# Scores of two differential heads in one group of matmuls, dilated projections cut into six halves, on one Trainium2 core

## The chip, the cores and the metric

The kernel runs on one core of one Trainium2 chip. The metric is the device time of one execution in microseconds (us): the median of several executions, beside which one execution was recorded by the hardware profiler. All times below of "the trace" come from that one recorded execution.

## What is computed

One decoder block over 256 tokens of width 1024 (all float32): attention with sixteen heads of two kinds, and then a mixture of 32 experts with the top four chosen for each token. Cut to what matters here:

```
h = rms_norm(x); proj = h @ w_in                      # 1024 x 3072
dq, dk, dv, lq, lk, lv = split(proj)                  # six parts of 512 columns
# eight differential heads: two score maps each, contraction over 32
s = q[h, m] . k[h, m] / sqrt(32) - slope * dist ; causal
p = softmax(s[m=0]) - lam * softmax(s[m=1]) ; o = p @ dv ; rms_norm(o)
# eight dilated heads: one map each, contraction over 64, three dilations mixed
o = mixture(softmax(lq . lk)) @ lv
x = x + mix @ w_out
x = x + moe(rms_norm(x))    # 32 experts: gate/up 1024 x 2048, down 1024 x 1024
return rms_norm(x)
```

The expert weights are 32 x 12.6 MB; every one of them is read once.

## The kernel before, in words

**Stages.** After the normalised input is turned (`hT`), TensorE makes the query/key part of the differential heads (`project(DQK, k)`, k from 0 to 7), then the differential values (`DV`). Then a loop over steps g = 0 to 15 runs heads 0 to 7 (differential) and 8 to 15 (dilated), with the rest of the projections (`EQ`, `EK`, `EV`: the dilated queries, keys and values) and later pieces of the output projection put between the small matmuls of the heads as filling. After step 15 come the rest of the output projection, the router and the experts, two experts to a round.

**One step on TensorE** (the loop near the end of the attention part of the TensorE program). Step g turns the probabilities of head g-1 (`turn_probs`, three transposes), makes the scores of head g+1 (`score(g + 1)`, for the differential heads), does its filling from the table `FILL`, turns a pair of mixed heads where g is 4, 6, 8 or 10 (`turn_mix`), and multiplies the probabilities of head g-1 with the values (`pv`). A step is named below by its g.

**The scores.** `score(g)` makes the two maps m = 0, 1 of one head. A map has 256 query rows in two parts: the later 128 against 256 keys and the earlier 128 against 128 keys. Its operands lie in 32 partitions, 64*(g % 2) + 32*m and on, so the two maps use two of the four groups of 32 rows of the array; they go to banks 4 and 5 of PSUM, for every head. Dilated heads go in twos already (`score_pair`: two heads, 64 partitions each, banks 4 and 5).

**VectorE, iteration g:** `negated_scores(g + 1)` reads the scores of the next head out of PSUM, adds the distance term and takes the row minimum; `diff_probs(g)` normalises the exponentials of head g and subtracts the second map; then come odd tasks: `rest_of_bias(1)` and `bias_part(1)` (two long operations that split the expert biases into bf16 parts, in iterations 1 and 2; their end, `bias_split`, lets the load queue start the loads of `w_out`), `keep_qk` (copies two finished 128x256 pieces of a projection out of PSUM with the scale), and `norm_pair` in iterations 3, 5, 7, 9 (normalises a pair of heads before `turn_mix`; it has one operation on GpSimd in its middle).

**ScalarE, iteration g:** `turn_probs(g - 1)` copies the turned probabilities, `exps(g + 1)` makes the exponentials, `keep_mixT` copies the turned pair, `keep_pv` the head's output. For g of 4, 6 and 8 `keep_mixT` stands after `exps(g + 1)`. On TensorE `pv` of the same step waits for that copy (`mixT_ready`), since both use bank 7.

**The load queue (SyncE)** issues all weight loads in the order of the program, each after a wait for its buffer. `gu_ring` has sixteen slots; during attention `w_in` lies in slots 0 to 11 and `hT`, `qkT`, `vS` in 12 to 15. The loads of the first two experts' gate/up weights go in eight steps s, which wait in order: dqk_used 2 and 4, then (after `bias_split` and the loads of `w_out`) eq_used 2 and 4, ev_used 2 and 4, ev_used 4 with scores_done 8, and, for s = 7, all scores, the turned pairs and the values' use. After it come the first down weights, which wait for the output projection.

## Time and profile before

| what | us |
|---|---|
| median of 3 executions (lowest, highest) | 1057.95 (1056.53, 1058.64) |
| the profiled execution | 1058.58 |
| its span in the trace | 1056.9 |
| TensorE matmul busy | 1037.4 |
| VectorE / ScalarE / GpSimd busy | 231.4 / 118.0 / 21.6 |
| moved by the DMA engines | 423.87 MB, 401 GB/s over the span |

The span is the time between the first and the last record of the core; 1.7 us of the execution lie around it. Matmuls overlap in the array, so the start of one record to the start of the next tells what a matmul costs, and not its length. Each float32 matmul of the program stands in the trace as two records of the same shape. In the views "<-" behind a wait names what ended it.

### The profile page before, as it was taken

How to read it: one execution, taken by the hardware profiler on the slowest of the kernel's cores; microseconds unless marked ns; L12 is line 12 of the kernel's file. 1: busy time of each engine (PE TensorE's matmuls, PEld its weight loads, DVE VectorE, ACT ScalarE, POOL GpSimd, SP SyncE). 2: the span in 40 equal slices, each digit the busy share in tenths (PEclk: the TensorE clock that was granted, in tenths of full speed). 3: DMA queues.
4: the chain of work that ended last, by engine and by line, in shares of the span. 5: the costliest groups of instructions: out<-in, count | busy, mean ns of one | idle time of the engine just before them, and what ended most of it. 6: DMA issues, size and time to landing. Idle time of an engine off the chain costs nothing.

```text
span 1056.9 us, 13197 instructions
## 1 busy us (share of the span) xinstructions
PE 1037.4 (98%) x5569; PEld 464.8 (44%) x5569; DVE 231.4 (22%) x515; ACT 118.0 (11%) x275; POOL 21.6 (2%) x39
## 2 busy tenths in 40 slices
PE   8999999999999999999999999999999999999997
PEld 7686544434343433434343434343433434343432
DVE  3567543121111111112121211111111111121111
ACT  1133420010000000000000000000000000000001
POOL 1000410000000000000000000000000000000000
PEclk9999999999999999999999999999999999999999
DMA  9946669999999999999999999999999999999996
GB/s 289 417 180 245 235 267 380 426 428 427 434 430 432 431 430 429 434 434 429 433 430 434 429 433 432 434 429 434 430 434 428 434 430 434 425 425 429 427 422 258
DMA packets 28027, 423.87 MB, mean 401 GB/s; under 512 B 5392, under 2 KB 5408, under 8 KB 11008
## 3 DMA queue, kind: packets, MB, share of 16 engines
q1 hardware_dynamic: 25680, 422.80, 94.7%
q10 hardware_dynamic: 2320, 0.67, 0.3%
q8 instruction: 21, 0.34, 0.1%
q14 instruction: 6, 0.05, 0.0%
HBM read 422.41 MB, written 1.05 MB: 401 GB/s over the span
## 4 chain that ended last, share of the span: by engine, by line
PE 90%; DVE 7%; ACT 1%; issue 1%; DMA 1%; SPq 0%; DVEq 0%; POOL 0%
PE psum L953 42%; PE psum L1001 15%; PE psum L1023 7%; PE psum L673 6%; PE psum L915 5%; PE psum L1040 4%; PE psum L788 3%; PE psum L648 3%; PE psum L678 2%; DVE mixed L1448 2%; DVE mixed L1444 2%; DVE mixed L1446 2%; ACT mixed L580 1%; PE psum L939 1%; DMA gu_ring<-in_w_in_dram 1%
## 5 line engine op out<-in xcount | busy, mean ns | idle before, releaser
L953 PE MATMUL psum<-gu_ring,mixed 128*64 128x512 f32 x2048 | 446.1, 593 | 0.0
L953 PEld LDWEIGHTS psum<-gu_ring,mixed 128*64 128x64 f32 x2048 | 143.4, 137 | 280.8 <-issue 275.7
L1444 DVE TENSOR_SCALAR mixed<-psum 128x512 f32<-128x512 f32 x32 | 22.1, 692 | 379.7 <-PE psum L953 379.7
L1001 PE MATMUL psum<-dn_ring,mixed 128*64 128x512 f32 x352 | 78.0, 595 | 3.8 <-ACT mixed L580 3.8
L1001 PE MATMUL psum<-mixed 128*64 128x512 f32 x352 | 78.0, 595 | 0.0
L1401 DVE TENSOR_TENSOR mixed<-posm,iota 128x256 f32<-128x256 f32 x47 | 20.0, 425 | 258.8 <-PE psum L648 258.5
L934 PE MATMUL psum<-mixed 64*128 64x512 f32 x256 | 63.6, 615 | 0.7 <-ACT mixed L584 0.7
L598 ACT ACTIVATE mixed<-psum 128x512 f32<-128x512 f32 x30 | 17.9, 597 | 402.1 <-PE psum L953 402.1
L673 PE MATMUL psum<-gu_ring 128*128 128x256 f32 x256 | 59.2, 389 | 1.8 <-DMA gu_ring<-in_w_in_dram 1.8
L915 PE MATMUL psum<-mixed,xres 128*128 128x128 f32 x480 | 57.4, 278 | 0.0
L915 PEld LDWEIGHTS psum<-mixed,xres 128*128 128x128 f32 x480 | 55.0, 192 | 0.7
L673 PEld LDWEIGHTS psum<-gu_ring 128*128 128x128 f32 x256 | 49.1, 195 | 9.7 <-issue 2.5
L584 ACT ACTIVATE mixed<-psum 128x512 f32<-128x512 f32 x32 | 19.1, 597 | 274.4 <-PE psum L1001 191.9
L1040 PE MATMUL psum<-ident,mixed 128*64 128x64 f32 x704 | 47.1, 286 | 2.0
L1001 PEld LDWEIGHTS psum<-dn_ring,mixed 128*64 128x64 f32 x352 | 25.1, 137 | 52.3 <-issue 52.3
L1040 PEld LDWEIGHTS psum<-ident,mixed 128*64 128x64 f32 x704 | 44.1, 216 | 8.5 <-DVE mixed L1448 8.5
L1001 PEld LDWEIGHTS psum<-mixed 128*64 128x64 f32 x352 | 24.3, 137 | 45.3 <-issue 44.0
L934 PEld LDWEIGHTS psum<-mixed 64*128 64x128 f32 x256 | 22.0, 186 | 41.8 <-issue 40.2
L1023 PE MATMUL psum<-dn_ring,mixed 128*64 128x512 f32 x160 | 35.4, 595 | 0.5
L1023 PE MATMUL psum<-mixed 128*64 128x512 f32 x160 | 35.4, 595 | 0.5 <-ACT mixed L580 0.5
L1414 DVE TENSOR_TENSOR mixed<-psum,prm 128x512 f32<-128x512 f32 x28 | 19.4, 692 | 69.6 <-PE psum L915 69.6
L648 PEld LDWEIGHTS psum<-ident,mixed 128*128 128x128 f32 (+1 forms) x163 | 19.3, 160 | 34.8 <-issue 28.9
(162 smaller groups left out, 546.5 us busy)
## 6 DMA issues: line engine op xcount, KB each, us to landing
gu_ring<-in_w_gate_up_dram SPq DMA_DIRECT2D x44, 4096.0 KB, 34.2
gu_ring<-in_w_gate_up_dram SPq DMA_DIRECT2D x35, 2048.0 KB, 18.9
dn_ring<-in_w_down_dram SPq DMA_DIRECT2D x11, 4096.0 KB, 31.7
mixed<-in_w_down_dram SPq DMA_DIRECT2D x11, 4096.0 KB, 31.4
dn_ring<-in_w_down_dram SPq DMA_DIRECT2D x9, 2048.0 KB, 17.5
mixed<-in_w_down_dram SPq DMA_DIRECT2D x8, 2048.0 KB, 16.0
gu_ring<-in_w_in_dram SPq DMA_DIRECT2D x11, 1024.0 KB, 17.7
gu_ring<-in_w_gate_up_dram SPq DMA_DIRECT2D x9, 1024.0 KB, 8.5
```

The source lines that it names most:

```text
L648: return nc.tensor.transpose(dst, src, ident[0:rows, 0:rows])
L673: last = mm(bank[b][:, c:c + T], w[:, P * (m0 + m):P * (m0 + m + 1)], hT[:, k, :], start=(k == 0 and m % 2 == 0), stop=(k == KT - 1), skip ...
L678: last = mm(bank[b0 + a][:, :], hT[:, k, P * a:P * (a + 1)], w[:, v0:v0 + 512], start=(k == 0), stop=(k == KT - 1))
L788: last = mm(bank[2 * a + c][:, :], mixT[:, kt, P * a:P * (a + 1)], dn_ring[:, kt // 2, w0:w0 + 512], start=(kt == 0), stop=(kt == KT - 1))
L915: last = mm(bank[b][:, c:c + P], rows, sel[:, a, :, :].rearrange("p e n -> p (e n)"), start=(a == 0), stop=(a == TT - 1))
L934: last = mm(bank[(0, 5)[a] + c][:, :], combT[rows, P * a:P * (a + 1)], yrow[rows, :], start=False, stop=True, skip_group_check=True)
L953: last = mm(bank[b0 + b][CAP * c:CAP * (c + 1), :], xg[:, k, CAP * half:CAP * (half + 1)], gu_ring[:, 8 * half + k, w0:w0 + 512], start=Fa ...
L1001: last = mm(bank[4][CAP * c:CAP * (c + 1), :], actT[:, CAP * k:CAP * (k + 1)], dn_whole[half][:, k // 2, w0:w0 + 512], start=False, stop=( ...
L1023: last = mm(bank[4][CAP * c:CAP * (c + 1), :], actT[:, a0:a0 + CAP], dn_slot[slot][:, k // 2 % 2, w0:w0 + 512], start=False, stop=(k == KT ...
L1040: last = mm(bank[7][rows, CAP * k:CAP * (k + 1)], act_t.rearrange("n (p k) -> n k p", k=KT)[:, k, :], ident[:, rows], start=True, stop=True)
L1444: chain(V.tensor_scalar(up_t, bank[b0 + 1][:, :], 1.0 - LIMIT, 1.0 + LIMIT, ALU.max, ALU.min))
L1446: chain(V.scalar_tensor_tensor(out=up_t, in0=bank[b0][:, :], scalar=LIMIT, in1=up_t, op0=ALU.min, op1=ALU.mult))
```

## The change

Scores: `score(g)` is replaced by `score_maps(g)`, which makes heads g and g+1 (g even) in one go: four maps at partitions 0, 32, 64 and 96, the even head in banks 4 and 5, the odd one in banks 2 and 3, first the four wide parts and then the four narrow ones. It is called before `DV` 2 for heads 0 and 1, and in steps 1, 3 and 5. `score_maps(0)` waits for all four `keep_qk` of the differential part. `negated_scores` reads banks 2 and 3 for odd heads.

Projections: `EQ`, `EK` and `EV` are each cut into two halves h (two of four pieces, or one of two token blocks), all eight k of a half before the other half, half 0 in bank 0 and half 1 in bank 1; banks 2 and 3 are no longer used by them. A unit of filling is half a k; the units per step are 8, 6, 6, 6, 6, 4, 6, 6 for steps 1 to 8, twice the former numbers. The matmuls are the same in number and size. VectorE copies the four halves of `EQ` and `EK` one by one in iterations 2, 3, 4 and 6 (before: two in 4, two in 6), in iteration 3 ahead of `norm_pair`.

Biases: `rest_of_bias(1)` and `bias_part(1)` both go to iteration 0 of VectorE; in iteration 1 it waits for its own probabilities there.

Mix: ScalarE does every `keep_mixT` ahead of `exps(g + 1)`.

```diff
-        FILL = {0: [(DV, k) for k in range(4, KT)], 1: [(EQ, 2), (EQ, 3)], 2: [(EQ, 4), (EQ, 5), (EQ, 6)],
-                3: [(EQ, 7), (EK, 0), (EK, 1)], 4: [(EK, 2), (EK, 3), (EK, 4)], 5: [(EK, 5), (EK, 6), (EK, 7)],
-                6: [(EV, 0), (EV, 1)], 7: [(EV, 2), (EV, 3), (EV, 4)], 8: [(EV, 5), (EV, 6), (EV, 7)]}
+        HALVES = [(c, h, k) for c in (EQ, EK, EV) for h in range(2) for k in range(KT)]
+        FILLED = (0, 0, 8, 14, 20, 26, 32, 36, 42, 48)
...
-                if g in TURN_AT and g > NH:
+                if g in TURN_AT:
                     keep_mixT(TURN_AT[g])
                 if g + 1 < 2 * NH:
                     exps(g + 1)
                 if g == 0:
                     keep_v(dv_done, 1, 6, 0)
-                if g in TURN_AT and g <= NH:
-                    keep_mixT(TURN_AT[g])
...
+            def project_half(chunk, h, k):
+
+                g = (1, 2, 2)[chunk]
+                w = gu_ring[:, 4 * g + k // 2, D * (k % 2):D * (k % 2) + D]
+                if chunk == EK and h == 0 and k % 2 == 0:
+                    pe.wait_ge(w_in_in[4 * g + k // 2], 16)
+                if k == 0:
+                    pe.wait_ge(qk_ready, ((1, 3), (5, 6), (7, 8))[chunk][h])
+                if chunk == EV:
+                    last = mm(bank[h][:, :], hT[:, k, P * h:P * (h + 1)], w[:, 512:D], start=(k == 0), stop=(k == KT - 1))
+                else:
+                    for m in range(2):
+                        c = (512, 0)[chunk] + P * (2 * h + m)
+                        last = mm(bank[h][:, T * m:T * (m + 1)], w[:, c:c + P], hT[:, k, :], start=(k == 0 and m == 0),
+                                  stop=(k == KT - 1), skip_group_check=True)
+                if h == 1 and chunk != EK:
+                    if k % 2:
+                        last.then_inc({EQ: eq_used, EV: ev_used}[chunk], 1)
+                elif k == KT - 1:
+                    last.then_inc(half_done, 1)
...
-            def score(g):
-                if g in (0, 4):
-                    pe.wait_ge(qk_ready, {0: 2, 4: 4}[g])
-                if g >= 1:
+            def score_maps(g):
+
+                if g == 0:
+                    pe.wait_ge(qk_ready, 4)
+                else:
                     pe.wait_ge(scores_read, g)
-                h = g % NH
-                for m in range(2):
-                    r0 = HD * (h % 2) + DK * m
-                    q, k = qkT[r0:r0 + DK, h // 2, :], qkT[r0:r0 + DK, 4 + h // 2, :]
-                    mm(bank[4 + m][:, 0:T], q[:, P:T], k, start=True, stop=True)
-                    last = mm(bank[4 + m][:, T:T + P], q[:, 0:P], k[:, 0:P], start=True, stop=True)
-                last.then_inc(scores_done, 1)
+                maps = [(bank[(4, 2)[i] + m], HD * i + DK * m) for i in range(2) for m in range(2)]
+                q, k = qkT[:, g // 2, :], qkT[:, 4 + g // 2, :]
+                for b, r in maps:
+                    mm(b[:, 0:T], q[r:r + DK, P:T], k[r:r + DK, :], start=True, stop=True)
+                for i, (b, r) in enumerate(maps):
+                    last = mm(b[:, T:T + P], q[r:r + DK, 0:P], k[r:r + DK, 0:P], start=True, stop=True)
+                    if i % 2:
+                        last.then_inc(scores_done, 1)
...
-            score(0)
-            project(DV, 2)
-            project(DV, 3)
+            score_maps(0)
+            for k in range(2, KT):
+                project(DV, k)
             for g in range(2 * NH):
+                fill = HALVES[FILLED[g]:FILLED[g + 1]] if g <= NH else []
                 if g == 1:
-                    pe.wait_ge(qk_ready, 3)
-                    project(EQ, 0)
-                    project(EQ, 1)
+                    for chunk, h, k in fill[0:4]:
+                        project_half(chunk, h, k)
+                    fill = fill[4:]
                 if g >= 1:
                     turn_probs(g - 1)
-                if g + 1 < NH:
-                    score(g + 1)
+                if g % 2 and g + 1 < NH:
+                    score_maps(g + 1)
                 elif g % 2 and g + 1 < 2 * NH:
                     score_pair(g + 1)
...
-                maps, b = (2, 4) if g < NH else (1, 4 + g % 2)
+                maps, b = (2, 4 - 2 * (g % 2)) if g < NH else (1, 4 + g % 2)
...
+                if g == 0:
+                    rest_of_bias(1)
+                    bias_part(1).then_inc(bias_split, 1)
                 if g == 1:
-                    rest_of_bias(1)
+                    dve.wait_ge(probs_ready, g + 1)
                 if g == 2:
-                    bias_part(1).then_inc(bias_split, 1)
                     dve.wait_ge(sub_in, 16 * 2)
                     V.tensor_scalar(prm[:, 16:17], prm[:, 16:17], 1.0 - LAM_INIT, None, ALU.mult).then_inc(sub_ready, 1)
-                if g == NH - 2:
-                    dve.wait_ge(ek_done, 1)
-                    for h in range(2):
-                        keep_qk(12 + 2 * h, 2 + h, 1.0)
+                if g in (2, 3, 4, 6):
+                    h = (2, 3, 4, 6).index(g)
+                    if h == 1:
+                        dve.wait_ge(eq_used, 4)
+                    else:
+                        dve.wait_ge(half_done, (1, 0, 2, 3)[h])
+                    keep_qk(8 + 2 * h, h % 2, HD ** -0.5 if h < 2 else 1.0)
                 if g >= 3 and g % 2 == 1 and g <= NH + 1:
                     norm_pair((g - 3) // 2)
-                if g == 4:
-                    dve.wait_ge(eq_used, 4)
-                    for h in range(2):
-                        keep_qk(8 + 2 * h, h, HD ** -0.5)
```

## Rows read from the trace of the kernel before

**Rows 1.** Busy time by stretch: stretch, us, busy PE PEld DVE ACT POOL, PEclk, DMA share, GB/s

```profile
42.00:112.00 70.00, 69.39 (x333) 49.21 (x333) 45.10 (x109) 24.71 (x88) 6.04 (x7) 1.00 0.62 254
...
124.60:139.50 14.90, 14.90 (x68) 7.27 (x67) 7.74 (x34) 4.95 (x13) 6.61 (x10) 1.00 0.01 2
139.50:163.00 23.50, 22.73 (x132) 11.99 (x134) 12.96 (x46) 4.39 (x11) 1.14 (x2) 1.00 0.90 358
182.00:1026.00 844.00, 836.77 (x4614) 341.51 (x4612) 129.92 (x244) 65.88 (x127) 0.00 (x0) 1.00 1.00 430
```

**Rows 2.** TensorE's records in order: start, length, line, shape, count; one round

```profile
801.18 13.95 PE L953 MATMUL psum<-gu_ring,mixed 128*64 128x512 f32 x64
...
857.71 0.65 PE L953 MATMUL psum<-gu_ring,mixed 128*64 128x512 f32 x2
```

**Rows 3.** Waits of the weight loads, 900 us to the end: in total, times, longest

```profile
PEld psum L953 <- DMA gu_ring<-in_w_gate_up_dram: 1.9, 4, 0.7
```

**Rows 4.** The load queue's issues in order of time

```profile
72.18 2.04 SPq L299 DMA_DIRECT2D dn_ring<-in_w_out_dram  x4
...
139.52 0.33 SPq L281 DMA_DIRECT2D gu_ring<-in_w_gate_up_dram  x1
...
162.25 2.04 SPq L331 DMA_DIRECT2D gu_ring<-in_w_gate_up_dram  x2
```

**Rows 5.** TensorE's records in order, steps 5 to 8 of the attention

```profile
85.10 0.50 PE L648 MATMUL psum<-ident,mixed 128*128 128x128 f32 x3
85.53 0.71 PE L720 MATMUL psum<-gu_ring 32*128 32x256 f32 x4
86.06 0.39 PE L721 MATMUL psum<-gu_ring 32*128 32x128 f32 x4
86.39 5.45 PE L673 MATMUL psum<-gu_ring 128*128 128x256 f32 x24
...
92.28 0.50 PE L648 MATMUL psum<-ident,mixed 128*128 128x128 f32 x3
...
95.61 1.88 PE L678 MATMUL psum<-gu_ring 128*128 128x512 f32 x4
98.10 0.41 PE L754 MATMUL psum<-gu_ring,mixed 128*128 128x64 f32 x2 [0.61 <-ACT mixed L528]
...
98.79 0.50 PE L648 MATMUL psum<-ident,mixed 128*128 128x128 f32 x3
...
105.94 0.50 PE L648 MATMUL psum<-ident,mixed 128*128 128x128 f32 x3
106.27 1.88 PE L678 MATMUL psum<-gu_ring 128*128 128x512 f32 x4
```

**Rows 6.** TensorE's records of the router, four groups of 32 columns

```profile
146.43 0.67 PE L845 MATMUL psum<-mixed 128*32 128x128 f32 x16
147.02 1.13 PE L788 MATMUL psum<-dn_ring,mixed 128*128 128x512 f32 x2
```

**Rows 7.** VectorE's records in order, iterations 1 and 2

```profile
59.27 0.95 DVE L1211 SCALAR_TENSOR_TENSOR mixed<-mixed,psum 128x768 f32<-128x768 f32 x1 [7.79 <-PE psum L721]
...
63.15 3.35 DVE L1183 TENSOR_TENSOR dn_ring<-dn_ring,mixed 32x3072 f32<-32x3072 f32 x1
...
70.41 1.75 DVE L1188 CAST mixed<-dn_ring 32x3072 bf16<-32x3072 f32 x1
```

**Rows 8.** VectorE's records in order, iterations 5 and 6

```profile
86.51 0.95 DVE L1211 SCALAR_TENSOR_TENSOR mixed<-mixed,psum 128x768 f32<-128x768 f32 x1 [2.37 <-PE psum L721]
...
92.47 0.42 DVE L1259 TENSOR_TENSOR mixed<-mixed,st 128x256 f32<-128x256 f32 x1 [1.12 <-POOL st L432]
93.70 0.95 DVE L1211 SCALAR_TENSOR_TENSOR mixed<-mixed,psum 128x768 f32<-128x768 f32 x1 [0.81 <-PE psum L721]
...
97.19 0.35 DVE L1229 SCALAR_TENSOR_TENSOR mixed<-mixed,st 128x128 f32<-128x128 f32 x1
97.46 1.28 DVE L1176 SCALAR_TENSOR_TENSOR gu_ring<-psum,mixed 128x512 f32<-128x512 f32 x2
```

More of the change, by code:

```diff
@@ L241, in moe_block @@
         PAIR_AT = {11: 4, 13: 5, 15: 6}
[L242 to L245 removed]
+        DQK, DV = range(2)
+        EQ, EK, EV = range(3)
+        HALVES = [(c, h, k) for c in (EQ, EK, EV) for h in range(2) for k in range(KT)]
+        FILLED = (0, 0, 8, 14, 20, 26, 32, 36, 42, 48)
         OUT = {9: [(0, 1), (0, 0)], 10: [(1, 0)], 11: [(2, 0)], 12: [(3, 0)], 13: [(1, 1)], 14: [(4, 0)], 15: [(5, 0)]}
@@ L666, in project @@
                     pe.wait_ge(w_in_first[k], 16)
-                elif chunk in (DQK, DV, EK) and k % 2 == 0:
+                elif k % 2 == 0:
                     pe.wait_ge(w_in_in[s], 16)
-                if chunk in (DQK, EQ, EK):
-                    b0, m0, n = {DQK: (0, 0, 8), EQ: (0, 4, 4), EK: (2, 0, 4)}[chunk]
-                    for m in range(n):
-                        b, c = b0 + m // 2, T * (m % 2)
-                        last = mm(bank[b][:, c:c + T], w[:, P * (m0 + m):P * (m0 + m + 1)], hT[:, k, :],
+                if chunk == DQK:
+                    for m in range(KT):
+                        b, c = m // 2, T * (m % 2)
+                        last = mm(bank[b][:, c:c + T], w[:, P * m:P * (m + 1)], hT[:, k, :],
@@ L674, in project @@
                                   start=(k == 0 and m % 2 == 0), stop=(k == KT - 1), skip_group_check=True)
+                    if k % 2:
+                        last.then_inc(dqk_used, 1)
                 else:
-                    b0, v0 = {DV: (6, 0), EV: (0, 512)}[chunk]
                     for a in range(TT):
-                        last = mm(bank[b0 + a][:, :], hT[:, k, P * a:P * (a + 1)], w[:, v0:v0 + 512],
-                                  start=(k == 0), stop=(k == KT - 1))
-                if chunk in (DQK, EQ, EV) and k % 2:
-                    last.then_inc({DQK: dqk_used, EQ: eq_used, EV: ev_used}[chunk], 1)
@@ L682, in project @@
-                if chunk == DV and k == KT - 1:
-                    last.then_inc(dv_done, 1)
-                if chunk == EK and k == KT - 1:
-                    last.then_inc(ek_done, 1)
+                        last = mm(bank[6 + a][:, :], hT[:, k, P * a:P * (a + 1)], w[:, 0:512], start=(k == 0),
+                                  stop=(k == KT - 1))
+                    if k == KT - 1:
+                        last.then_inc(dv_done, 1)
+            def project_half(chunk, h, k):
[13 more added lines that the diff above has]
+                if h == 1 and chunk != EK:
+                    if k % 2:
+                        last.then_inc({EQ: eq_used, EV: ev_used}[chunk], 1)
+                elif k == KT - 1:
+                    last.then_inc(half_done, 1)
@@ L800, in _ @@
             project(DV, 1)
-            score(0)
-            project(DV, 2)
-            project(DV, 3)
+            score_maps(0)
+            for k in range(2, KT):
+                project(DV, k)
             for g in range(2 * NH):
+                fill = HALVES[FILLED[g]:FILLED[g + 1]] if g <= NH else []
                 if g == 1:
-                    pe.wait_ge(qk_ready, 3)
-                    project(EQ, 0)
-                    project(EQ, 1)
+                    for chunk, h, k in fill[0:4]:
+                        project_half(chunk, h, k)
+                    fill = fill[4:]
                 if g >= 1:
                     turn_probs(g - 1)
-                if g + 1 < NH:
-                    score(g + 1)
+                if g % 2 and g + 1 < NH:
+                    score_maps(g + 1)
                 elif g % 2 and g + 1 < 2 * NH:
                     score_pair(g + 1)
-                for i, (chunk, k) in enumerate(FILL.get(g, ())):
-                    if k == 0:
-                        pe.wait_ge(qk_ready, {EK: 4, EV: 6}[chunk])
-                    project(chunk, k)
-                    if i == 0 and g in TURN_AT:
+                for i, (chunk, h, k) in enumerate(fill):
+                    project_half(chunk, h, k)
+                    if i == 1 and g in TURN_AT:
                         turn_mix(TURN_AT[g], g)
```

6 lines of the change are left out of this document (2 added, 4 removed).

## The prediction

> **What bounds the kernel now.** I read the busy time by stretch first. From 42 to 112 us, where the heads and projections run, TensorE is busy for 69.39 of 70 us at the full clock, and VectorE for 45 [rows 1]: what is taken off TensorE's list there is time. Then the question is whether the end follows. From 182 to 1026 us both TensorE (836.8 of 844) and the DMA engines (share 1.00, 430 GB/s) are full [rows 1]. A round of two experts reads 2 x 12.58 = 25.17 MB, which is 58.5 us at 430 GB/s; TensorE's rounds are 857.71 - 801.18 = 56.5 us apart [rows 2]. So the stream of weights is slower by 2.0 us a round and uses up the lead that it had, and after 900 us weight loads begin to wait for data (1.9 us in four waits) [rows 3]. The end is therefore the start of the stream plus its bytes. Where does the stream start? From 124.6 to 139.5 us the DMA engines stand still (share 0.01) [rows 1]; the next load is issued at 139.52 and waits for TensorE's scores, turned pairs and values, and those behind it up to 162.25 wait for TensorE's output projection and first expert [rows 4]. So a microsecond that TensorE saves before 139 us is saved in both, and only such a one.
>
> **Scores, eight times two maps against four times four.** Step 5 begins with turned probabilities at 85.10 and scores at 85.53, and its filling starts at 86.39: 1.29 us. Step 8 has no scores, and its filling starts 106.27 - 105.94 = 0.33 us after its beginning [rows 5]. One call of scores thus costs 0.96 us, two calls 1.92. What would four maps together cost? Filling records of 256 columns come at about 0.22 us each, transposes of 128 columns at 0.11 (three in 0.33) [rows 5]. A call has four records of 256 and four of 128 columns, 1.32 us if one ran after the other; the 0.96 is half of it (0.66) and 0.30 for entering and leaving. So two groups of 32 rows already run at once. Four maps are 2.64 us of records: 0.66 + 0.30 = 0.96 with four at once (and some 0.03 for two more starts), 1.32 + 0.30 = 1.62 with two at once, 2.94 with one at a time. The trace has no four groups of rows. Its nearest row is the router's sixteen records of 128 columns in four groups of columns: 1.76 us in series, 147.02 - 146.43 = 0.59 us in fact, which is four at once (0.44) and 0.15 [rows 6]. There the four write different partitions; here they write the same partitions in four banks, as the two do now in two banks. I take four at once, 0.99 us: 4 x (1.92 - 0.99) = **3.7 us saved**. The bounds are 1.2 us saved (two at once) and 4.1 us lost (one at a time).
>
> The Trainium skill (TensorE: Matmul & The Clock Gate, section "Measured speedup vs the span model") gives 3.07 times for four row tiles with a contraction over 32 and 512 columns. By it a group would be 2.64 / 3.07 + 0.30 = 1.16 us and the saving an estimated 3.0 us; no run here shows that yet.
>
> **Mix copied sooner.** In step 6 the last filling starts at 95.61, four records of 0.43 us, so `pv` could start at 97.33; it starts at 98.10, after a wait for ScalarE's copy of the turned pair (L528) [rows 5], which stands behind the exponentials. With the copy first, 0.8 us goes. The exponentials are then later by the wait for the turn, in steps 4, 6 and 8. They are those of head g+1, whose probabilities are turned in step g+2; a step is 4.7 to 7.2 us, and this delay some 3. No cost. Bounds: 0 (the next wait is as late) and 0.8.
>
> **Halves.** The records are the same in number and shape, and each step has the same amount of filling: zero on TensorE. New are the waits. Each half's first k waits for a copy of the same bank, made one to three iterations before (qk_ready 5 in iteration 2, used in the middle of step 3; 6 in 3, used late in step 4; 7 in 4, used in step 6). VectorE in turn waits for a half in iterations 2, 3, 4 and 6, with `norm_pair` and the next scores queued behind it, and TensorE's `turn_mix` behind those. In iteration 3 the half's last record is 1.7 us into the filling and VectorE comes to the wait some 5 us after its scores, so that costs nothing but the copy's 0.65 us ahead of `norm_pair`; `turn_mix` has over 0.5 us left. The load queue now gets eq_used and ev_used from the second half alone. Its loads of s = 4 to 6 are then issued between 103 and 108 us, and they land long before 135 us, since the engines idle now from 124.6 us [rows 1]. Zero, within 0.3 us both ways.
>
> **Biases.** 3.35 + 1.75 us of VectorE [rows 7] go to iteration 0. They are hidden by the 7.79 us in which it waits for the scores of head 2 [rows 7]; without that cover they would push head 1's probabilities and cost up to 5 us. The loads of `w_out` are issued at about 57 us and not at 72.18 [rows 4]; nobody waits for them. Taking them out of iterations 1 and 2 gives nothing on TensorE. `score_maps(0)` waits for four copies and not two; that is 1.28 us more at most [rows 8], and two k of `DV` (eight records of 0.43, 3.4 us) stand before it on TensorE to cover all four. Zero.
>
> **What is late next.** The shorter steps must still find their probabilities. The tight place is step 7. Count from step 5's beginning, 85.10: VectorE begins with the scores at +1.41 and ends `norm_pair` at 92.89 = +7.79; head 6's probabilities take 97.54 - 93.70 = 3.84 more: +11.65 [rows 8]. TensorE needs 7.2 for step 5 and 6.51 - 0.96 - 0.8 = 4.75 for step 6, +11.95 [rows 5]. The fourth copy (half of 1.28 us, begun 3.76 after the scores, +12.2) is wanted by `score_pair(8)` at +12.4 [rows 8]. Both hold by 0.2 to 0.3 us, about a semaphore's way; I take off 0.1 us. In iteration 4 and 6 VectorE needs no new scores, so it is earlier there than now.
>
> **The sum.** 3.7 + 0.8 - 0.1 = 4.4 us. The profiled execution took 1058.58 us (0.6 above the median of 1057.95), of which 1054.2 remain; against the median that is 1053.6 us. All steps from 7 on, the stream and the end move by the same amount, since each is released by TensorE.
>
> **Rivals.** (A) Only two groups of rows run at once: 1.2 + 0.8 - 0.1 = 1.9 us, **1056.1**. For it: no row shows more than two row groups. The Trainium skill (PSUM — Partial Sum Buffer, section "PSUM: the matmul accumulator") says that TensorE's only way out is one write port to PSUM; read strictly that would forbid even the two banks at once of now. Chance 0.14. (B) The hand-offs come due: VectorE is late by about 1 us at the beginnings of steps 2 and 7, where its margin is 0.2 us: 2.4 us remain, **1055.6**. Against it: two of its iterations are about 11 us of work and TensorE's two steps 13. Chance 0.08. (C) TensorE is earlier but the stream isn't, because a load behind 139.52 is bound to something that doesn't move: the 2 us a round eat the gain, **1058.0**. The idle 14.9 us speak against it [rows 1]. Chance 0.06. (D) Slower: the four groups block each other at PSUM and run one after the other. Then a group is 2.94 us, 4 x 1.02 = 4.1 lost, 0.8 won: **1061.3**. It turns the sign once a group is over 2.1 us, and is beyond 0.2% slower from 2.65. The two at once of now speak against it. Chance 0.04. The forecast has 0.68.
>
> **Chances and range.** 0.2% is 2.1 us, about what can be told from no change. The forecast is faster by more in nearly all its cases (0.67), A in under half (0.06), B mostly (0.06): faster 0.79. Within: the rest of these and C, 0.16. Slower: D and a remainder, 0.05. The range goes from 1052.4 (the forecast less the 1.2 us by which the executions differ) to 1056.8 (A with its spread); it leaves C and D out.
>
> **What would show it.** Right: four records of 256 columns within some 50 ns of each other, a group of scores under 1.1 us from its first record to the filling, four such groups; no wait for L528 in step 6 and step 6 near 4.7 us; step 8 begins near 101.5 (now 105.94); the load of 139.52 issued near 135.1; the same 430 GB/s and the same round after it. Wrong: a group of 1.6 us or more; idle time of TensorE before the probabilities of head 1 or 6, or in front of `score_pair(8)`; a load issue between 135 and 160 us that kept its time.

## The result, and the profile after

| | before | after |
|---|---|---|
| median, us (lowest, highest; executions) | 1057.28 (1056.53, 1058.64; 4) | 1051.76 (1051.32, 1052.05; 4) |
| the profiled execution | 1058.58 | 1052.05 |
| its span | 1056.9 | 1050.3 |
| first score record | 42.10 | 40.31 |
| step 9 begins | 112.26 | 105.43 |
| load of s = 7 is issued | 139.52 | 132.70 |

The ratio of after to before is 0.995 [0.9938, 0.9962]: 5.5 us faster, where 4.4 was forecast; the time lies 0.6 us under the range. The seven loads before s = 7 come earlier too.

The comparison of two profiled executions holds more than the change. The first score record starts 1.8 us earlier (42.10 and 40.31), and nothing ahead of it was changed. What the change does is counted from there: from the first score to the beginning of step 9 it was 70.16 us and is 65.12, so **5.04 us** less. The experiments below show that both pass on to the end, the sum of the two meeting the difference of the spans to within 0.4 us.

Stretches of after (columns as in [rows 1], whose stretches these are):

```profile
42.00:112.00 70.00, 70.00 (x344) 49.23 (x343) 48.05 (x123) 28.27 (x96) 7.51 (x9) 1.00 0.66 268
124.60:139.50 14.90, 14.90 (x57) 7.13 (x56) 5.21 (x18) 4.07 (x9) 3.79 (x7) 1.00 0.39 144
182.00:1026.00 844.00, 836.80 (x4614) 341.53 (x4610) 129.89 (x244) 65.25 (x126) 0.00 (x0) 1.00 1.00 430
```

TensorE has no idle time left among the heads (70.00 of 70). The DMA engines' gap has moved forward, so that they are at work again before 139.5. From 182 to 1026 us the two kernels' lines are nearly the same: TensorE has the same 4614 records and 836.8 us, the DMA engines move the same 430 GB/s, and only ScalarE's time differs by 0.6 us. Nothing was gained or lost there.

TensorE's records of after in order (start, length, line, shape, count), steps 1 to 3:

```profile
55.04 0.49 PE L646 MATMUL psum<-ident,mixed 128*128 128x128 f32 x3
55.46 0.71 PE L734 MATMUL psum<-gu_ring 32*128 32x256 f32 x8
55.99 0.40 PE L736 MATMUL psum<-gu_ring 32*128 32x128 f32 x8
56.32 3.72 PE L693 MATMUL psum<-gu_ring 128*128 128x256 f32 x16
...
60.49 0.50 PE L646 MATMUL psum<-ident,mixed 128*128 128x128 f32 x3
60.83 5.35 PE L693 MATMUL psum<-gu_ring 128*128 128x256 f32 x24
66.01 0.33 PE L770 MATMUL psum<-gu_ring,mixed 128*128 128x64 f32 x2
...
66.62 0.49 PE L646 MATMUL psum<-ident,mixed 128*128 128x128 f32 x3
67.05 0.71 PE L734 MATMUL psum<-gu_ring 32*128 32x256 f32 x8
```

L734 and L736 are the wide and the narrow parts of `score_maps`. Eight wide records take 0.71 us from the first one's start to the last one's end, as long as four did in step 5 of before. The first records of the four maps' wide parts start within 0.02 us of each other (55.456 to 55.476). The group takes 56.32 - 55.46 = 0.86 us up to the filling, as a call of two maps did (86.39 - 85.53 = 0.86) [rows 5]. Four maps cost what two cost. Step 2, now without scores, is 6.13 us long and was 7.18. The other steps with a call taken out went from 7.41 to 6.36 (step 4) and from 6.51 to 4.61 (step 6); steps 1, 3, 5, 7 and 8 kept their length to within 0.02.

The same view of after, steps 6 and 7:

```profile
87.35 0.50 PE L646 MATMUL psum<-ident,mixed 128*128 128x128 f32 x3
87.69 1.88 PE L689 MATMUL psum<-gu_ring 128*128 128x512 f32 x4
89.41 0.38 PE L646 MATMUL psum<-ident,mixed 128*128 128x128 f32 x2
89.62 1.88 PE L689 MATMUL psum<-gu_ring 128*128 128x512 f32 x4
91.34 0.33 PE L770 MATMUL psum<-gu_ring,mixed 128*128 128x64 f32 x2
...
91.96 0.50 PE L646 MATMUL psum<-ident,mixed 128*128 128x128 f32 x3
92.39 0.70 PE L747 MATMUL psum<-gu_ring 64*128 64x256 f32 x4
```

`pv` (L770) starts 1.72 us after the last filling's beginning, which is its four records of 0.43, without the wait for L528 that stood there before [rows 5]. In step 7 the turned probabilities of head 6 and the scores (L747) follow at once: neither has an idle time in front. The margin is small, though. One of the waits of TensorE's weight loads from 40 to 112 us of after (in total, times, longest):

```profile
PEld psum L747 <- DVE gu_ring L1191: 0.2, 1, 0.2
```

The weight load of these scores waited 0.2 us for VectorE's copy of the last half of `EK`; it runs beside the matmuls, so nothing was lost.

The load queue (start of the first, time to the end of the last, count):

```profile
101.36 31.67 SPq L281 DMA_DIRECT2D gu_ring<-in_w_gate_up_dram  x4
134.54 0.33 SPq L290 DMA_DIRECT2D dn_ring<-in_w_down_dram  x1
```

The four issues are those of s = 4 to 7; the last begins at 101.36 + 31.67 - 0.33 = 132.70, 6.8 us earlier than the 139.52 of [rows 4], and the span ends 6.6 us earlier.

### The profile page after: what moved, and what is told of

Same layout as the page of the kernel before. It is cut to its first block, busy times and chain, and to the rows that moved or that the text cites. A ratio compares the mean times of both kernels' runs of the same rounds, so it can differ in the third digit from the quotient of the medians.

```text
span 1050.3 us, 13196 instructions
## 1 busy us (share of the span) xinstructions
PE 1032.3 (98%) x5569; PEld 461.9 (44%) x5569; DVE 231.3 (22%) x515; ACT 118.0 (11%) x275; POOL 21.6 (2%) x39
## 3 DMA queue, kind: packets, MB, share of 16 engines
HBM read 422.41 MB, written 1.05 MB: 403 GB/s over the span
## 4 chain that ended last, share of the span: by engine, by line
PE 86%; DVE 6%; DMA 5%; SPq 1%; ACT 1%; issue 1%; DVEq 0%; POOL 0%
PE psum L968 40%; PE psum L1016 15%; PE psum L1038 5%; PE psum L930 5%; PE psum L1055 5%; DMA gu_ring<-in_w_gate_up_dram 4%; PE psum L804 3%; PE psum L693 3%; PE psum L669 3%; PE psum L646 2%; DVE mixed L1463 2%; DVE mixed L1459 2%; DVE mixed L1461 2%; PE psum L689 1%; PE psum L675 1%; SPq L384 1%
## 5 line engine op out<-in xcount | busy, mean ns | idle before, releaser
L646 PE MATMUL psum<-ident,mixed 128*128 128x128 f32 (+1 forms) x163 | 31.7, 294 | 1.5 <-DVE mixed L1345 0.5
L954 PE MATMUL psum<-mixed 96*64 96x512 bf16 x192 | 32.7, 392 | 0.0
```

The lines of the kernel that those rows point to most:

```text
L646: return nc.tensor.transpose(dst, src, ident[0:rows, 0:rows])
L954: return mm(bank[b][CAP * c:CAP * (c + 1), :], bias_sel[half][0:3 * NE, :], bias3[0:3 * NE, col:col + 512], start=True, stop=False, skip_g ...
```

## Experiments: does it repeat, and what is each part worth?

Each result is given with the kernel before, run in turn with it on the same chip; all changes are to the changed kernel, unless said. "Heads" is the time from the first score record to the beginning of step 9 in the profiled execution, "start" the time from the span's beginning to that record.

| run | median, us | ratio to before | span | start | heads |
|---|---|---|---|---|---|
| before (profile of the start) | | | 1056.9 | 42.10 | 70.16 |
| e0 changed | 1051.13 | 0.9948 [0.9935, 0.9962] | 1049.3 | 39.57 | 65.13 |
| e10 changed again | 1051.50 | 0.9954 [0.9940, 0.9967] | 1049.4 | 39.66 | 65.12 |
| e1 head by head | 1051.53 | 0.9948 [0.9933, 0.9964] | 1051.8 | 41.97 | 65.18 |
| e2 mix late | 1054.20 | 0.9972 [0.9960, 0.9984] | 1052.5 | 41.80 | 66.11 |
| e3 one head a step | 1055.65 | 0.9993 [0.9984, 1.0002] | 1053.4 | 39.42 | 69.27 |
| e4 biases late | 1052.47 | 0.9961 [0.9945, 0.9976] | 1050.5 | 39.56 | 66.35 |
| e5b extra in step 6 | 1054.72 | 0.9981 [0.9972, 0.9990] | 1052.9 | 39.59 | 68.56 |
| e6 less gather | 1051.32 | 0.9954 [0.9940, 0.9967] | 1049.3 | 39.96 | 65.13 |
| e7 filler | 1051.86 | 0.9953 [0.9940, 0.9967] | 1049.4 | 39.73 | 65.13 |
| e9 more filler | 1052.06 | 0.9956 [0.9942, 0.9969] | 1051.2 | 41.14 | 65.14 |
| e8 mix sooner alone (on before) | 1056.18 | 0.9997 [0.9988, 1.0006] | 1053.9 | 39.54 | 69.75 |

**The changed kernel once more.**

> The changed kernel again, beside the kernel before on the same chip. Two theories of the 5.5 us between the medians (and 6.6 between the two spans). Theory 1: the heads' part gives 4.9 us (in the two traces, from the first record of DV to the beginning of step 9: 112.26 - 38.57 = 73.7 before, 105.59 - 36.95 = 68.6 or a little more after), and the rest, up to 1.8 us, lies before the first changed line and comes and goes between executions: in the trace of before TensorE's granted clock is 0.5 from 8.5 to 12.0 us, in that of after it is not. Then executions of one kernel fall into two groups some 1.7 us apart, each with its clock share (about 0.997 against 0.999), and like against like the change is 4.9 to 5.2 us. Theory 2: the change itself moves the start; then all executions of this kernel start fast and all of the kernel before start slow, and the difference is 6.6 us in each round.

Measured: 1051.13 us (1051.05 to 1051.69) beside 1056.64 for the kernel before (17 executions, 1056.14 to 1057.37). The heads took the same 65.1 us, but the start was 39.57 and not 40.31, and the span 1049.3.

Between the profile of before and this one the span differs by 7.6 us: 42.10 - 39.57 = 2.53 of it is the start, and 70.16 - 65.13 = 5.03 the heads. The two terms add up to the whole. In the runs below the same sum comes out to within 0.4 us. None of the executions of either kernel here is late, and their medians still differ by 5.5 us; of this the trace explains the 5.03 of the heads, and the rest is inside the interval of the ratio. So the theory that the change itself moves the start is out: before's code also starts at 39.54 (e8).

**The order of the maps in the queue.** Here head g's eight records are issued before head g+1's.

```diff
-                for b, r in maps:
-                    mm(b[:, 0:T], q[r:r + DK, P:T], k[r:r + DK, :], start=True, stop=True)
-                for i, (b, r) in enumerate(maps):
-                    last = mm(b[:, T:T + P], q[r:r + DK, 0:P], k[r:r + DK, 0:P], start=True, stop=True)
-                    if i % 2:
-                        last.then_inc(scores_done, 1)
+                for pair in (maps[0:2], maps[2:4]):
+                    for b, r in pair:
+                        mm(b[:, 0:T], q[r:r + DK, P:T], k[r:r + DK, :], start=True, stop=True)
+                    for b, r in pair:
+                        last = mm(b[:, T:T + P], q[r:r + DK, 0:P], k[r:r + DK, 0:P], start=True, stop=True)
+                    last.then_inc(scores_done, 1)
```

> The same sixteen records of a group, but the two maps of the even head first (wide, then narrow) and then those of the odd head. If the array takes whatever rows are free out of its queue, the two heads still overlap and a group costs 0.9 us: 0 us against the changed kernel. If only neighbours in the program run at once, two maps run at a time and a group costs some 0.65 us more: 4 x 0.65 = 2.6 us slower than the changed kernel (about 1054.3 where that has 1051.7).

Measured: 1051.53 us; heads 65.18. TensorE's records of this kernel, step 1:

```profile
57.12 0.73 PE L735 MATMUL psum<-gu_ring 32*128 32x256 f32 x8
57.66 0.41 PE L737 MATMUL psum<-gu_ring 32*128 32x128 f32 x8
58.00 2.21 PE L693 MATMUL psum<-gu_ring 128*128 128x256 f32 x9
```

A group is 58.00 - 57.12 = 0.88 us, 0.02 more than in the order of the change. So the order of the maps is worth next to nothing as long as the sixteen records stand together. What a matmul of another kind between the two heads' maps would do, no run shows. The span, 1051.8, is 2.5 longer than e0's, and 2.40 of it is a later start, not the order.

**Mix copied late again.**

```diff
-                if g in TURN_AT:
+                if g in TURN_AT and g > NH:
                     keep_mixT(TURN_AT[g])
                 if g + 1 < 2 * NH:
                     exps(g + 1)
                 if g == 0:
                     keep_v(dv_done, 1, 6, 0)
+                if g in TURN_AT and g <= NH:
+                    keep_mixT(TURN_AT[g])
```

> Only the copy of the turned pair goes back behind the exponentials. Theory 1 (its wait in step 6 was worth 0.8 us and stays of that size): +0.8 us against the changed kernel, step 6 of 5.4 us and not 4.6. Rival: in the changed kernel the exponentials of head 7 are ready earlier, since their scores are there a step sooner, so the copy is no longer late: 0 us.

Measured: 1054.20 us (six executions, five of them 1054.2 to 1054.6, one 1051.85). Step 6 is 5.60 us and not 4.61, every other step is the same. TensorE's waits from 40 to 112 us of this kernel (in total, times, longest); there is only one:

```profile
PE psum L772 <- ACT mixed L528: 0.8, 1, 0.8
```

Its place among TensorE's records of the same kernel, in order:

```profile
91.11 1.88 PE L691 MATMUL psum<-gu_ring 128*128 128x512 f32 x4
93.75 0.41 PE L772 MATMUL psum<-gu_ring,mixed 128*128 128x64 f32 x2 [0.75 <-ACT mixed L528]
```

So in the changed kernel the sooner copy is worth 0.98 us, as the first theory had it, a little more than the 0.8. The span is 3.2 us longer than e0's: 2.23 from the start, 0.98 from the heads. Five of the six executions lie with a late start; one does not, and that one is 0.7 us above e0's median. Nothing ahead of the first score differs from e0, and why so many of this run's executions start late is not shown; the ratio in the table holds both parts.

**One head a step.** The halves, the biases and the mix stay; the scores go back to one head a call.

```diff
-                maps = [(bank[(4, 2)[i] + m], HD * i + DK * m) for i in range(2) for m in range(2)]
+                maps = [(bank[(4, 2)[g % 2] + m], HD * (g % 2) + DK * m) for m in range(2)]
...
+                if k == 4:
+                    score_maps(1)
                 project(DV, k)
...
-                if g % 2 and g + 1 < NH:
+                if g and g + 1 < NH:
                     score_maps(g + 1)
```

> Everything of the change (halves, biases, copy, banks) but the grouping: the scores of one head at a time, one head a step as before. Theory 1 (grouping is the source; a call taken out is worth 1.05 us): 4 x 1.05 = 4.2 us slower than the changed kernel, so some 0.8 us faster than the kernel before. Rival (halves or earlier biases brought part of it): 2 to 3 us slower than the changed kernel only.

Measured: 1055.65 us, ratio 0.9993 [0.9984, 1.0002]; heads 69.27, that is 4.14 more than e0. TensorE's records of this kernel, step 2, which can be laid beside step 2 of after above:

```profile
60.63 0.50 PE L646 MATMUL psum<-ident,mixed 128*128 128x128 f32 x3
61.05 0.70 PE L734 MATMUL psum<-gu_ring 32*128 32x256 f32 x4
61.59 0.39 PE L736 MATMUL psum<-gu_ring 32*128 32x128 f32 x4
61.91 5.45 PE L693 MATMUL psum<-gu_ring 128*128 128x256 f32 x24
67.19 0.33 PE L770 MATMUL psum<-gu_ring,mixed 128*128 128x64 f32 x2
```

Two things cost here. From the turned probabilities to the filling it is 61.91 - 60.63 = 1.28 us with scores and 60.83 - 60.49 = 0.34 without: 0.94. And the same 24 records of filling take 67.19 - 61.91 = 5.28 us after scores, but 66.01 - 60.83 = 5.18 without them: another 0.10, on the first record behind the scores (lengths 5.45 and 5.35). Together 1.04. The steps say the same: 7.17 against 6.13, 7.41 against 6.35, 5.66 against 4.61, and 1.04 in the prologue. Four calls are 4.2 us by the steps and 4.14 by the heads. The span is 4.1 above e0's: nearly the heads alone, as the start is the same within 0.15. The steps also show what the rest of the change does without the grouping: steps 2 to 5 are as long as in before, and step 6 is 0.85 shorter, which is the mix.

**Biases late.** The two long operations of VectorE go back to iterations 1 and 2, and the wait that the change put into iteration 1 goes.

```diff
-                if g == 0:
+                if g == 1:
                     rest_of_bias(1)
+                if g == 2:
                     bias_part(1).then_inc(bias_split, 1)
-                if g == 1:
-                    dve.wait_ge(probs_ready, g + 1)
-                if g == 2:
                     dve.wait_ge(sub_in, 16 * 2)
```

> The changed kernel with the two long bias operations of VectorE back in iterations 1 and 2. Theory 1 (the move is worth nothing by itself, since VectorE had room): 0 us, the first scores to step 9 in 65.2 us. Rival (with shorter steps VectorE no longer has room in iteration 1, and head 2's probabilities come late): step 3 begins 0.5 to 2 us later, and the end with it.

Measured: 1052.47 us; heads 66.35, 1.2 more than e0, and the span 1.2 longer. The first theory (0 us) was wrong; the rival came. VectorE's records of this kernel in order, iterations 1 and 2:

```profile
59.55 3.35 DVE L1198 TENSOR_TENSOR dn_ring<-dn_ring,mixed 32x3072 f32<-32x3072 f32 x1
62.93 0.95 DVE L1226 SCALAR_TENSOR_TENSOR mixed<-mixed,psum 128x768 f32<-128x768 f32 x1
...
66.42 0.35 DVE L1244 SCALAR_TENSOR_TENSOR mixed<-mixed,st 128x128 f32<-128x128 f32 x1
66.81 1.75 DVE L1203 CAST mixed<-dn_ring 32x3072 bf16<-32x3072 f32 x1
```

TensorE's records of the same kernel, end of step 2 and beginning of step 3:

```profile
65.64 0.39 PE L772 MATMUL psum<-gu_ring,mixed 128*128 128x64 f32 x2
66.83 0.55 PE L646 MATMUL psum<-ident,mixed 128*128 128x128 f32 x3 [0.80 <-DVE mixed L1244]
```

The bias operation holds back head 3's row minima and then head 2's probabilities (ready at 66.77); step 3 begins at 66.83, where e0, whose first score is at the same time to 0.01 us, is at 65.88. That is 0.95 of the 1.2 us; steps 3 and 4 have the rest (7.24 and 6.57, in e0 7.19 and 6.35). Step 2 was 7.18 us in before, and VectorE could take 3.35 us more in it; in 6.13 us it cannot. Where the grouped scores shorten a step, the biases must leave.

**Mix sooner, on the kernel before.** The same order of ScalarE as in the change, nothing else.

```diff
-                if g in TURN_AT and g > NH:
+                if g in TURN_AT:
                     keep_mixT(TURN_AT[g])
                 if g + 1 < 2 * NH:
                     exps(g + 1)
                 if g == 0:
                     keep_v(dv_done, 1, 6, 0)
-                if g in TURN_AT and g <= NH:
-                    keep_mixT(TURN_AT[g])
```

> The kernel before, with nothing changed but ScalarE's copy of the turned pair ahead of the exponentials. Theory 1 (parts add): step 6 shorter by 0.85 us (6.51 to 5.66), all other steps as before, the end 0.8 to 0.9 us earlier. Rival (the exponentials that are now later make another step late): a step from 5 to 8 grows, gain 0 to 0.3 us.

Measured: 1056.18 us beside 1056.57, ratio 0.9997 [0.9988, 1.0006], so no difference that can be told; by the trace the heads are 69.75 us, 0.41 less than before. The parts did not add: another step grew, as the rival had it (its gain of 0 to 0.3 us is 0.41 here). Step 6 lost 0.85 us (6.51 to 5.66), step 7 gained 0.42 (7.15 to 7.57). VectorE's copies of this kernel in iteration 6:

```profile
94.91 1.28 DVE L1174 SCALAR_TENSOR_TENSOR gu_ring<-psum,mixed 128x512 f32<-128x512 f32 x2
```

TensorE's records of the same kernel, step 7:

```profile
95.39 0.50 PE L646 MATMUL psum<-ident,mixed 128*128 128x128 f32 x3
96.24 0.70 PE L729 MATMUL psum<-gu_ring 64*128 64x256 f32 x4 [0.36 <-DVE gu_ring L1174]
```

`score_pair(8)` (L729) now waits for the second of the two copies that `keep_qk` makes in iteration 6. In the changed kernel only one half of `EK` is left to copy there; VectorE's record of after:

```profile
91.62 0.68 DVE L1191 SCALAR_TENSOR_TENSOR gu_ring<-psum,mixed 128x512 f32<-128x512 f32 x1
```

It ends at 92.30, and the scores of dilated heads 8 and 9 start at 92.39. e3 bears this out: it has the sooner mix and the halves with one head a step, and there step 6 is 5.66 us as here, but step 7 is 7.15 and not 7.57. (It also has the biases early; they are 30 us ahead of this place.) So the parts of the change do not add: about half of the mix's gain is given back in step 7 where the halves are missing. A run of the changed kernel without the halves was not made.

## Experiments: does a microsecond of the heads reach the end, and what about one of the rounds?

**Work added in step 6.** Four more matmuls of 512 columns, which are eight records; the sum in their bank is started anew behind them.

```diff
                 if chunk == EV:
+                    for _ in range(4 if h == 0 and k == 0 else 0):
+                        mm(bank[h][:, :], hT[:, k, P * h:P * (h + 1)], w[:, 512:D], start=True, stop=True)
                     last = mm(bank[h][:, :], hT[:, k, P * h:P * (h + 1)], w[:, 512:D], start=(k == 0), stop=(k == KT - 1))
```

> The changed kernel with eight more records of 512 columns (3.44 us of TensorE) in step 6, in front of the first EV half. Theory 1 (before 139 us TensorE's time goes through to the stream's start and to the end one to one): +3.4 us against the changed kernel; the load of s = 7 is issued 3.4 us later. Rival C of the prediction (the stream's start does not follow TensorE): well under 3 us, most of it taken back after 140 us.

Measured: 1054.72 us (10 executions, 1054.2 to 1055.2) beside 1056.62; e0 was 1051.13.

```profile
86.97 3.60 PE L690 MATMUL psum<-gu_ring 128*128 128x512 f32 x8
90.41 1.88 PE L691 MATMUL psum<-gu_ring 128*128 128x512 f32 x4
```

The eight records take 90.41 - 86.97 = 3.44 us, step 6 is 8.04 and not 4.61, the load of s = 7 is issued at 135.4 and not at 132.0 (e0), and the span is 3.6 us longer. What TensorE does before the load of s = 7 passes to the end, within 0.2 us one to one.

**Work taken away in the rounds.** In four of the rounds the gather uses one of its two token blocks, so that part of the expert input is missing there.

```diff
-                    for a in range(TT):
+                    for a in range(1 if half_only else TT):
...
-                    gather(j + 2, turned)
+                    gather(j + 2, turned, half_only=loaded is not None)
```

> The changed kernel with half of the gather left out in rounds 0, 1, 2 and the last but one (only the first 128 tokens are gathered for the next round's experts, so those results lack the rest): sixteen matmul records fewer each time, 4 x 1.9 = 7.5 us less TensorE after the stream has started, 5.7 of them near 200 to 320 us. Theory 1 (the end is the stream's start plus its bytes): 0 us, at most 1 us faster; TensorE waits for weights the more at the end. Rival (TensorE sets the end alone, and the stream follows it): 7 us faster.

Measured: 1051.32 us, span 1049.3 as in e0: nothing gained (its start is 0.39 later, so 0.4 us at most). The gather's records go from 480 to 416; at 0.11 us each [rows 5] that is 7 us of TensorE, most of it before 360 us. The waits of the weight loads for gate/up data, 900 us to 1050, in this kernel (in total, times, longest):

```profile
PEld psum L968 <- DMA gu_ring<-in_w_gate_up_dram: 13.0, 11, 2.4
```

The same in e0:

```profile
PEld psum L968 <- DMA gu_ring<-in_w_gate_up_dram: 1.4, 3, 0.6
```

What TensorE no longer computes it waits. The stream of weights sets the end, and the heads count because they set when it starts.

## Experiments: the start

The profiled execution of before is late by 2.5 us at its first score beside e0, and nothing before that place was changed. The busy time of before by stretch (columns as in [rows 1]):

```profile
8.00:10.00 2.00, 1.71 (x5) 1.42 (x6) 0.00 (x0) 1.28 (x4) 0.00 (x0) 0.64 1.00 408
10.00:12.00 2.00, 2.00 (x7) 1.58 (x5) 0.00 (x0) 0.00 (x0) 0.00 (x0) 0.51 1.02 414
12.00:14.00 2.00, 2.00 (x11) 1.77 (x10) 0.00 (x0) 0.00 (x0) 0.00 (x0) 1.00 1.03 424
```

TensorE's records of before, in order, up to the first projection:

```profile
5.83 0.66 PE L648 MATMUL psum<-ident,xres 128*128 128x128 f32 x4
8.29 6.03 PE L673 MATMUL psum<-gu_ring 128*128 128x256 f32 x19 [1.81 <-DMA gu_ring<-in_w_in_dram]
```

The same stretches of after:

```profile
8.00:10.00 2.00, 1.80 (x8) 1.63 (x9) 0.10 (x1) 2.00 (x4) 0.00 (x0) 1.00 1.03 418
10.00:12.00 2.00, 2.00 (x11) 1.76 (x10) 0.00 (x0) 0.04 (x1) 0.00 (x0) 1.00 1.02 418
```

TensorE's records of e0 up to the first projection (in after the wait there is 0.90 us):

```profile
6.36 0.66 PE L646 MATMUL psum<-ident,xres 128*128 128x128 f32 x4
7.43 4.80 PE L669 MATMUL psum<-gu_ring 128*128 128x256 f32 x21 [0.41 <-ACT gu_ring L482]
```

In before TensorE stood still for 1.81 us, waiting for the first piece of `w_in`, and its granted clock fell from full (2.4 GHz) to half (1.2 GHz) from 8.55 to 11.96 us, while it was computing again: 3.4 us at half speed, in 10.00 to 12.00 seven records and not eleven. The traces of e1 and e2 show the same fall (8.22 to 11.63 and 7.96 to 11.37, after 1.80 and 1.85 us of waiting), and their starts are 41.97 and 41.80. The other traces have none, and their starts lie between 39.42 and 40.31, but for e9's 41.14. There the first projection stands behind eight matmuls of filling and begins at 9.10; the clock first became full at 7.30 us (after: 7.00, with the projection at 8.20; e0: 6.09 and 7.43; e3: 4.39 and 7.31). So a late start costs 2.2 to 2.5 us against e0, and all of it arrives at the end. Not all of it is the clock's: the projection of before begins 0.86 us later than e0's (8.29 and 7.43), and 3.4 us at half speed are an estimated 1.7, together 2.56 where 2.53 was measured. For e1 and e2 the same sum gives 2.44 and 2.32, measured 2.40 and 2.23.

The executions of one kernel lie in two groups, some 1.4 to 2.5 us apart: of e1's four, three took 1051.1 to 1051.8 us and one 1053.5; of before's four in the result, two took 1056.5 and 1056.6, and two 1058.0 and 1058.6; of its 47 beside the experiments, three are over 1058. e3 has two such executions in ten, e6 one in five, e8 one in ten.

**Filler.** Does work in the gap keep the clock up? Four (e7) and eight (e9) matmuls into a free bank before the first projection; the diff is e7's, and e9 has range(8) in its place:

```diff
+            for i in range(4):
+                mm(bank[1][:, 0:P], posm[:, 0, 0:P], posm[:, 0, 0:P], start=True, stop=True)
             for k in range(KT):
```

> The changed kernel with four small matmuls (0.9 us at full clock) in TensorE's wait for the first weights, between the first transposes and the first projection. In the traces with a late start TensorE idles 1.8 us there and its clock is granted at 0.5 from about 8 to 11.5 us. Theory 1 (the idle time is what lets it fall): no execution starts late, all lie within 1 us of 1051.1, and the gain on a late one is 2.4 us. Rival (the fall has its own time, whatever TensorE does in that wait): late ones, near 1053.5, go on to occur; the fast ones 0 to 0.3 us slower.

> The changed kernel with eight small matmuls (1.75 us at full clock) in TensorE's wait for the first weights. In the traces with a late start that wait is 1.8 us long (0.4 to 1.3 us in those without), and the clock is granted at 0.5 after it. Theory 1 (the wait is what lets the clock fall): no late start in any execution, and the fast ones later by what the filling overshoots, 0.3 to 0.9 us. Rival: late ones (2 us above the others) occur as often as beside it.

> The changed kernel on the same chip as the one with eight small matmuls, to count late starts and to set their medians side by side. Theory 1: median near 1051.2, executions in two groups, one in five or so some 2 us above the others. Rival (the change does away with late starts): all within 1 us.

Measured: 1051.86 us with four (five executions, 1051.20 to 1051.89), 1052.06 with eight (1051.31 to 1052.93), 1051.13 and 1051.50 without (ten executions, 1051.05 to 1052.05). None of the ten with filler is as late as 1053.5, but neither is any of these ten without. Over all runs without filler, before and after in the result among them, 15 of 114 executions are late, and five of these 15 are e2's; at that rate none in ten is no surprise (a chance of about a quarter). So the filler's benefit is not shown. Its medians are 0.4 to 0.7 us higher, which is inside the intervals of the ratios; in e9's trace it delays the first projection. e6's trace had 1.68 us of waiting and no fall; what tips the clock one way or the other these rows do not tell. It stays open, and no version here beats the changed kernel.

## Why the prediction missed by 1.8 us, point by point

The mechanism was right. Two numbers were not: the base from which the gain was taken off (1.2 of the 1.8 us) and the price of a call of scores, 0.96 us in the prediction and 1.05 in the traces (most of the other 0.6).

- **What bounds the kernel: right.** "A microsecond that TensorE saves before 139 us is saved in both": e5b (3.43 added, 3.6 arrived), and the sums start + heads = span of e0, e1, e2 and e3. "The stream of weights is slower": e6. [rows 1] and [rows 2] were enough for it.
- **Scores: the mechanism was right, the term mis-sized.** 3.7 us was forecast, 4.2 came (4.19 from before to after, 4.14 from e3 to e0). The step that failed is "one call of scores thus costs 0.96 us". It was measured from the beginning of a step to the beginning of its filling [rows 5]; the price goes on for another 0.10 in the first record of the filling (0.32 us to the next one, 0.22 elsewhere), so a call taken out saves 1.05. And "some 0.03 for two more starts" was nothing: 0.86 before, 0.86 after. 4 x 0.09 + 4 x 0.03 = 0.48, the whole difference.
- The Trainium skill (TensorE: Matmul & The Clock Gate, section "Measured speedup vs the span model") gives 3.07 times for four row tiles. The trace agrees: the 16 records of a group are 2.64 us in series and 0.86 from the first record to the filling, and 2.64 / 0.86 = 3.07, though the widths here are 256 and 128 columns and the Trainium skill's is 512. The estimate of 3.0 us saved came out too low because 0.30 for entering and leaving was added on top (1.16 us a group); the 0.86 holds them already.
- **Mix: right, 0.85 where 0.8 was taken.** `pv` started 0.77 later than it could, and its first two records took 0.24 us and not 0.17 up to the next; before to e8 shows 0.85 in step 6. In the changed kernel undoing it costs 0.98 (e2): there the copy starts 4.31 us into step 6 (5.22 in before), 0.91 sooner, but `pv` could start 1.06 sooner, as the step has no scores. "Bounds: 0 (the next wait is as late)" was near the truth for the old kernel: there 0.42 of the 0.85 comes back in step 7 (e8).
- **Halves: right on zero** for steps 1, 3, 5, 7 and 8, and by e3 for 2 and 4. Their use was not seen as a whole: they take one of two copies out of `score_pair(8)`'s way, 0.42 us between e8 and e3.
- **Biases: a step that failed without touching the sum is "taking them out of iterations 1 and 2 gives nothing on TensorE".** Against the kernel before it is true: e3, which has the biases early and one head a step, keeps the 7.18 and 7.19 us of before's steps 2 and 3 (7.17 and 7.18). Against the change without this part it is false by 1.2 us (e4). The tight place at step 2 was weighed only in the rivals, with the biases already gone.
- **What is late next: no loss where 0.1 was taken off.** Step 7 began without a wait. Head 6's probabilities ended at 91.70, 0.26 ahead of it. The fourth copy ended at 92.30, only 0.09 ahead of `score_pair(8)`, whose weight load had waited 0.2 us for it. "About a semaphore's way" was too much for such a margin: where TensorE did wait for VectorE it started 0.05 to 0.06 us after the end of the work (e8: 96.19 and 96.24; e4: 66.77 and 66.83).
- **The sum.** 4.19 for the scores and 0.85 for the mix make 5.04, where 3.7 + 0.8 - 0.1 = 4.4 was forecast: 0.6 of the 1.8 us.
- **The base: the other 1.2 us.** The forecast was "against the median" of three executions, 1057.95. The profiled one with 1058.58 carries the late start, and by their times (1057.95 and 1058.64) two of those three do. Beside the experiments before's medians are 1056.57 to 1056.64, and 1056.6 - 5.0 = 1051.6 is close to the 1051.76 that came. The row that shows it, the granted clock of 0.51 from 10 to 12 us, was in the trace of before, 30 us ahead of the stretch that was read. "The forecast less the 1.2 us by which the executions differ" set the range's lower end from that high base, with nothing added for a term that was too small. That the time fell 0.6 us under the range is thus in part the luck of which executions were late.
- **Rivals.** A (two groups at once) would have had groups of 1.5 us or more; they have 0.86. B (VectorE late at steps 2 and 7): no wait at either, but it was near (in after, head 1's probabilities ended at 60.27 and step 2 began at 60.49). C (the stream keeps its time): the load of 139.52 moved with TensorE. D (slower, the four groups one after the other): the same 0.86. Four banks were written at the same time over the same partitions, as two were before; of the one write port that the Trainium skill names (PSUM — Partial Sum Buffer, section "PSUM: the matmul accumulator"), the trace shows no limit on these.
- **The signs.** All of those named for right came: wide parts within 0.02 us of each other, four groups of 0.86 us, step 6 of 4.61 us without a wait, the same round (56.5 us) and the same 430 GB/s. Step 8 (99.11) and the load of s = 7 (132.70) came 2.4 us earlier than named, 1.8 of it by the start.

## What to carry to other kernels

Before a forecast, compare the executions with each other and read the profile's first microseconds too: here a start that comes in two kinds shifts the base by 2.2 to 2.5 us, half of what the change moves. Take the price of a special piece of work from whole steps with it and without it (7.17 against 6.13), not from its own first record to its end, since it goes on in the record behind. And when a change shortens a step, count again what the other engines had room for in it: operations that were hidden (the biases, the second copy) come due, and parts of a change are worth different amounts together and alone (the mix 0.98 us, or 0.41).

## What the hardware showed that was not expected

- Four matmuls of 32 rows, next to each other in the queue, ran at once: 2.64 us of records in 0.86, entering and leaving included. Two at once had cost the same 0.86, so the second pair was free.
- The order among them did not matter: head by head (0.88) or all wide parts first (0.86).
- The first full-height matmul behind a group of 32-row matmuls costs 0.10 us more than it does elsewhere, on top of 0.94 up to it.
- Early in the execution, TensorE's granted clock fell to half for 3.4 us in three of thirteen traces, each after 1.80 to 1.85 us of standing still (a wait of 1.68 had no fall). These executions ended 2.2 to 2.5 us later than e0 by their start; the half speed is an estimated 1.7 of it, and the later first projection the rest.
